# Banded attention: the query norm factors of groups 1 to 3 by a power on GpSimd and a Newton step on VectorE

## Chip, cores and metric

The kernel runs on one core of one Trainium2 chip. The metric is the device time of one execution in microseconds; the time before is the median of 3 runs. Engines are named as the profile names them: PE (TensorE matmul), PEld (its weight loads), DVE (VectorE), ACT (ScalarE), POOL (GpSimd), SP (SyncE).

## What is computed

The reference is two transformer blocks over 512 tokens of 1024 features: eight stages, four of them gated feed-forward layers. The change lies in the seventh stage, a sliding-window attention. It has 16 query heads and 2 key heads of 64 features, and blocks of 128 queries that read their own and the previous key block. Cut to what matters:

```python
def rms_norm_2(x, g):
    xf = x.astype(jnp.float32)
    y = xf * lax.rsqrt(jnp.mean(xf * xf, axis=-1, keepdims=True) + EPS)
    return (y * g.astype(jnp.float32)).astype(x.dtype)

def swa_layer(x, norm_g, w_in, q_g, k_g, sinks, w_out):
    proj = rms_norm_2(x, norm_g) @ w_in
    q, k, v = jnp.split(proj, ...)
    q = rms_norm_2(q.reshape(B, S, C_KV_HEADS, C_GROUP, C_HEAD_DIM), q_g)
    k = rms_norm_2(k.reshape(B, S, C_KV_HEADS, C_HEAD_DIM), k_g)
    o = sliding_window_attention(q, k, v, sinks).astype(x.dtype)
    return x + o @ w_out
```

`sliding_window_attention` is scores, plus a bias by distance, softmax with a learned sink in the denominator, times values. The norm factor of a query and head, one over the root of its mean square, enters as a factor on its scores.

## The kernel before

All engines run hand-written, fixed instruction streams that are tied by semaphores. Nothing is reordered: the order in which each engine's function issues its work is the order in which it runs. Every large product is computed in three passes (high by high, low by high, high by low parts), one "unit" of weights of 128x1024 being eight tiles, 24 matmuls, some 5.5 us of PE. A unit's weights are loaded by SP, rounded to the high part by ACT (line 176) and the rest is formed on POOL (line 187), three units ahead of use.

The class `WindowAttention` (from line 2070 on) holds the stage. Its units are k, q0, q1, v, q2 to q7 and then eight units of the output projection. The attention itself runs in 16 steps (`STEPS`): step n is query block n % 4 of group n // 4, and a group is 4 heads, that is, two q tiles. A step's work goes around the engines:

- PE `scores(n)` (line 2182), two steps ahead of the rest;
- DVE `maxima(n)`: a copy of the sinks in the first two blocks of a group (line 2363), scores times norm factor plus bias, 4 instructions (line 2367), the negated maximum (line 2372);
- ACT `exps(n)`: 4 exponentials with their sums (line 2279);
- DVE `share(n)`: reciprocals of the sums (line 2380);
- POOL `divide(n)`: 4 products with these (line 2434);
- PE `turn_p(n)`: transposes into banks 6 and 7 (line 2196), ACT `copy_turned(n)` (line 2289), PE `values(n)` (line 2209);
- ACT `upper(n)` and DVE `lower(n)`: high and low part of the result (lines 2296 and 2386).

`maxima(13)`, to take one, waits for nothing but the scores, `exps(11)` and what stands ahead of it on DVE: in step 12 of the loop DVE issues `maxima(13)`, behind `share(11)` and `lower(7)` of step 11. Between these steps PE runs the projections q4 to q7 in steps 1, 3, 5 and 7 (`PROJECTED`); from step 8 on there is no projection, and PE gets the first tiles of the output projection only at step 14.

The norm factors of a group's queries take these steps. ACT squares the two q tiles (line 2263). In step 1, 5 and 9 (`STATS`) PE sums the squares by `query_stats(g)` for group g = 1, 2, 3 (line 2166), in a bank of PSUM of its own for g = 1 and in the free half of the bank of `values(n - 3)` for g = 2 and 3. One step later ACT takes the root (`query_roots`, line 2270) between `copy_turned` and `upper`, and DVE the reciprocal (`query_rstd`, line 2350), the last thing ahead of `maxima(4g)` in the next step. Square root and exponential are in different tables of ACT, so each of the three roots has a table load ahead of it and another ahead of the exponentials that follow. Group 0 has the same steps ahead of the loop, behind a root that the keys need anyway.

Four stages have constants of their own (masks, biases), which ACT's DMA queue loads at the stage's start, with one semaphore for each stage.

## Time and profile before

| | |
|---|---|
| median of 3 runs | 2199.66 us (2197.24 to 2201.47) |
| the profiled execution | 2197.87 us |
| its span, first to last instruction | 2196.1 us |
| PE busy | 2172.5 us, 99% of the span |
| DVE, ACT, POOL busy | 903.8, 839.2, 943.4 us |
| chain that ended last | PE 97%, DVE 1%, ACT 1% |
| granted clock of PE, mean | 0.997 |
| 16 steps of the attention | about 1703 to 1803 us of the span |

The profile is one execution. The median of the runs lies 1.8 us above the profiled execution's time, and that 1.8 us above its span. A busy share is an average over stages with different limits: what one stage is bound by is read in the timelines of that stage. "Idle before" in a timeline is the idle time of that engine ahead of the instruction, with the instruction that ended it.

### The profile page before, as it was taken

What the parts mean: (1) busy time and instruction counts of PE and PEld (TensorE: products, weight loads), DVE (VectorE), ACT (ScalarE), POOL (GpSimd) and SP (SyncE); (2) the same over time, 40 slices, a digit from 0 to 9 for tenths busy, and PEclk for the clock granted to TensorE, in tenths of its full rate; (3) what the DMA queues carried; (4) which work ended last, traced back from release to release, by engine and by line L of the source; (5) the groups of instructions that cost most, each with busy time, mean ns of one, the idle gap of its engine ahead of it and who ended that gap; (6) DMA issues with size and microseconds to landing.
All of it is one profiled execution on the core that took longest, in us unless ns stands there. A gap on an engine that the chain in (4) does not pass through costs nothing.

```text
span 2196.1 us, 28893 instructions
## 1 busy us (share of the span) xinstructions
PE 2172.5 (99%) x10346; PEld 1787.0 (81%) x10346; DVE 903.8 (41%) x1275; ACT 839.2 (38%) x1236; POOL 943.4 (43%) x457
## 2 busy tenths in 40 slices
PE   8999999999999999999999999999999999999999
PEld 7888887788887888888887788888888778888887
DVE  5222222554625522222226855555322655555400
ACT  5222223423433422223334634444323655444421
POOL 3444444423472444444442334444544435444443
PEclk9999999999999999999999999999999999999999
DMA  5333333222352233333332123333333103333332
GB/s 187 98 96 96 96 106 113 79 75 68 106 165 66 77 106 96 96 96 103 108 128 65 34 86 96 96 96 96 106 107 132 53 18 105 97 100 98 96 115 77
DMA packets 58973, 210.25 MB, mean 96 GB/s; under 512 B 6800, under 2 KB 7568, under 8 KB 58512
## 3 DMA queue, kind: packets, MB, share of 16 engines
q1 hardware_dynamic: 57024, 202.33, 30.4%
q10 hardware_dynamic: 1872, 6.83, 0.8%
q8 instruction: 55, 0.90, 0.2%
q14 instruction: 22, 0.18, 0.0%
HBM read 207.05 MB, written 2.10 MB: 95 GB/s over the span
## 4 chain that ended last, share of the span: by engine, by line
PE 97%; DVE 1%; ACT 1%; issue 0%; DMA 0%; POOL 0%; SPq 0%; DVEq 0%; ACTq 0%
PE psum L234 29%; PE psum L236 29%; PE psum L235 29%; PE psum L258 1%; PE psum L260 1%; PE psum L259 1%; PE psum L1286 1%; PE psum L1311 1%; PE psum L2196 1%; PE psum L2182 1%; PE psum L2209 1%; PE psum L1674 0%; PE psum L2166 0%; PE psum L841 0%; PE psum L1694 0%
## 5 line engine op out<-in xcount | busy, mean ns | idle before, releaser
L187 POOL TENSOR_TENSOR w_lo<-w_raw,w_hi 128x1024 fp32r<-128x1024 f32 x375 | 903.5, 2416 | 1151.8 <-ACT w_hi L176 1151.6
L234 PE MATMUL psum<-x_hi,w_hi 128*128 128x512 f32 x1816 | 713.9, 393 | 7.7 <-DVE x_lo L295 6.7
L236 PE MATMUL psum<-x_hi,w_lo 128*128 128x512 f32 x1816 | 707.9, 390 | 0.0
L235 PE MATMUL psum<-x_lo,w_hi 128*128 128x512 f32 x1816 | 707.6, 390 | 0.0
L176 ACT ACTIVATE w_hi<-w_raw 128x1024 fp32r<-128x1024 f32 x378 | 393.3, 1054 | 529.9 <-PE psum L236 496.4
L234 PEld LDWEIGHTS psum<-x_hi,w_hi 128*128 128x128 f32 x1816 | 340.8, 188 | 85.2 <-issue 10.6
L236 PEld LDWEIGHTS psum<-x_hi,w_lo 128*128 128x128 f32 x1816 | 340.7, 188 | 72.7
L235 PEld LDWEIGHTS psum<-x_lo,w_hi 128*128 128x128 f32 x1816 | 341.0, 188 | 70.5 <-issue 0.5
L279 DVE SCALAR_TENSOR_TENSOR x<-psum,x 128x512 f32<-128x512 f32 x64 | 44.3, 692 | 366.8 <-PE psum L236 366.2
L234 PE MATMUL psum<-ffn_hidden_hi,w_hi 128*128 128x512 f32 x352 | 136.9, 389 | 0.0
L235 PE MATMUL psum<-ffn_hidden_lo,w_hi 128*128 128x512 f32 x352 | 136.9, 389 | 0.0
L234 PE MATMUL psum<-glu_hidden_hi,w_hi 128*128 128x512 f32 x352 | 136.9, 389 | 0.0
L235 PE MATMUL psum<-glu_hidden_lo,w_hi 128*128 128x512 f32 x352 | 136.9, 389 | 0.0
L236 PE MATMUL psum<-ffn_hidden_hi,w_lo 128*128 128x512 f32 x352 | 136.9, 389 | 0.0
L236 PE MATMUL psum<-glu_hidden_hi,w_lo 128*128 128x512 f32 x352 | 136.9, 389 | 0.0
L564 ACT ACTIVATE ffn_hidden_hi<-row_d 128x512 f32 (+1 forms) x44 | 27.8, 632 | 222.3 <-DVE row_d L623 222.3
L612 DVE TENSOR_TENSOR row_d<-psum,rstd 128x512 f32<-128x512 f32 x44 | 30.4, 692 | 193.2 <-PE psum L236 193.1
L295 DVE SCALAR_TENSOR_TENSOR x_lo<-x,columns,x_hi 128x512 fp32r<-128x512 f32 x56 | 89.9, 1611 | 47.2 <-ACT x_hi L324 47.2
L558 ACT ACTIVATE row_d<-row_b,columns 128x512 f32<-128x512 f32 x44 | 36.0, 819 | 126.5 <-DVE row_b L612 126.5
L612 DVE TENSOR_TENSOR row_b<-psum,rstd 128x512 f32<-128x512 f32 x44 | 30.4, 692 | 130.0 <-PE psum L236 129.9
L235 PEld LDWEIGHTS psum<-ffn_hidden_lo,w_hi 128*128 128x128 f32 x352 | 66.1, 188 | 13.8
L236 PEld LDWEIGHTS psum<-glu_hidden_hi,w_lo 128*128 128x128 f32 x352 | 66.1, 188 | 13.8
(316 smaller groups left out, 2518.7 us busy)
## 6 DMA issues: line engine op xcount, KB each, us to landing
w_raw<-in_stream SPq DMA_DIRECT2D x378, 512.0 KB, 3.6
swa_bias<-in_swa_bias ACTq DMA_DIRECT2D x1, 2048.0 KB, 9.8
out<-x SPq DMA_DIRECT2D x8, 256.0 KB, 4.5
ab_bias<-in_ab_bias ACTq DMA_DIRECT2D x1, 1792.0 KB, 7.4
x<-in_x_in SPq DMA_DIRECT2D x5, 256.0 KB, 7.4
xattn_mem<-in_mem ACTq DMA_DIRECT2D x1, 1024.0 KB, 5.0
x<-in_x_in ACTq DMA_DIRECT2D x3, 256.0 KB, 4.8
w_raw<-in_stream SPq DMA_DIRECT2D x2, 256.0 KB, 3.9
```

What stands on the lines that cost most here:

```text
L176: act.activation(self.w_hi[:, place % SPLIT_SLOTS, :], self.w_raw[:, place % RAW_SLOTS, :], ACT.Copy).then_inc(self.w_hi_ready, 1)
L187: pool.tensor_tensor(self.w_lo[:, split, :], self.w_raw[:, raw, :], self.w_hi[:, split, :].bitcast(F32), ALU.subtract).then_inc(self.w_lo_ ...
L234: pe.matmul(out, w_hi, hi[:, k0 + j, :], start=first and j == order[0], stop=False)
L235: pe.matmul(out, w_hi, lo[:, k0 + j, :], start=False, stop=False)
L236: mm = pe.matmul(out, w_lo, hi[:, k0 + j, :], start=False, stop=last and j == order[-1])
L258: pe.matmul(out, hi[:, k, rows], w_hi, start=start, stop=False, skip_group_check=True)
L259: pe.matmul(out, hi[:, k, rows], w_lo, start=False, stop=False, skip_group_check=True)
L279: own(dve, dve.scalar_tensor_tensor(c.x[:, m, :], y, factor, c.x[:, m, :], ALU.mult, ALU.add), c.x_updated, self.done(m))
L295: dve.scalar_tensor_tensor(c.x_lo[:, m, :], c.x[:, m, :], self.gain_column(m), c.x_hi[:, m, :].bitcast(F32), ALU.mult, ALU.subtract).then_ ...
L558: act.activation(out[:], row[:, PAD:PAD + T], ACT.Identity, bias=self.table(f"f_conv_b{self.conv}", f, part * FT), scale=self.table(f"f_co ...
L564: act.activation(self.tile(self.h_hi, f), self.row3(c.row_d), ACT.Copy).then_inc(self.hidden_hi_ready, 1)
L612: own(dve, dve.tensor_tensor(up_row, up_bank, c.rstd[:], ALU.mult), self.up_scaled, f + (self.done + 1))
```

## The change

Group 0 keeps its root. For groups 1 to 3, at the place where DVE took the reciprocal, DVE now copies the sums plus epsilon from PSUM to a tile (`sums`), ahead of `lower`. POOL raises that tile to the power of -1/2 (`query_powers`) behind `divide` of the same step. At the start of the next step DVE makes one Newton step of it in three instructions, each waiting for the one before (`query_rstd`), ahead of `maxima(4g)`. ACT's `query_roots` for these groups goes. `upper` of the bank that holds the sums now waits for PE's sums to be done, which `query_roots` did before, and PE's `query_stats` of groups 2 and 3 waits for the previous factors. A tile of 128x16 is filled with -0.5 once. The four stages' constants count on one semaphore (32, 48, 112 and 128 are the running totals at 16 for each DMA); the loads themselves stay where they are.

```diff
+STAGE_LANDED = {"mix": 32, "xattn": 48, "ab": 112, "swa": 128}
...
-        self.consts = sem("consts_landed")
+        self.consts = c.stage_landed
...
+            self.q_power = sb("q_power", [P, 2, 2 * TB])
+            self.q_sums = sb("q_sums", [P, 2, 2 * TB])
...
             if g < 2:
                 turns.take(pe, f"qstat{g}")
+            else:
+                pe.wait_ge(self.q_rstd_ready, g)
...
-        def query_roots(g):
-            act.wait_ge(self.stat_done, 2 * g + 3)
-            if g >= 1:
-                act.wait_ge(self.q_rstd_ready, g)
-
-            act.activation(self.q_root[:], self.stat_columns(g)[:, 0:4 * TB].rearrange("p (t c) -> p t c", t=2),
-                           ACT.Sqrt, bias=self.eps64[:]).then_inc(self.root_ready, 1)
+        def first_roots():
+            act.wait_ge(self.stat_done, 3)
+            act.activation(self.q_root[:], self.query_sums(0), ACT.Sqrt, bias=self.eps64[:]).then_inc(self.root_ready, 1)
...
             act.wait_ge(self.values_done, n + 1)
+            if n > 0 and n + 3 in self.STATS:
+                act.wait_ge(self.stat_done, 2 * self.STATS[n + 3] + 3)
...
-            if n - 1 in self.STATS:
-                query_roots(self.STATS[n - 1])
...
+        def sums(g, bank_of):
+            dve.wait_ge(self.stat_done, 2 * g + 3)
+            if bank_of >= 0:
+                dve.wait_ge(self.mixed_hi_ready, bank_of + 1)
+            own(dve, dve.tensor_scalar(self.q_sums[:], self.query_sums(g), HALF * EPS, None, ALU.add),
+                self.q_sums_ready, g)
...
+            else:
+                dve.wait_ge(self.root_ready, g + 2)
+                chain.own(dve, dve.tensor_tensor(rstd, self.q_sums[:], self.q_root[:], ALU.mult))
+                chain.own(dve, dve.scalar_tensor_tensor(rstd, rstd, -0.5, self.q_root[:], ALU.mult, ALU.mult))
+                own(dve, dve.scalar_tensor_tensor(rstd, rstd, 1.5, self.q_root[:], ALU.add, ALU.mult),
+                    self.q_rstd_ready, g + 1)
...
+        chain.own(dve, dve.memset(self.q_power[:], -0.5))
...
         for n in range(self.STEPS):
+            if n - 2 in self.STATS:
+                query_rstd(self.STATS[n - 2])
             if n + 1 < self.STEPS:
                 maxima(n + 1)
             if n == 0:
                 take("q3", self.q[:, 3, :])
             share(n)
+            if n - 1 in self.STATS:
+                sums(self.STATS[n - 1], n - 4)
             if n >= 4:
                 lower(n - 4)
-            if n - 1 in self.STATS:
-                query_rstd(self.STATS[n - 1])
...
+        def query_powers(g):
+            pool.wait_ge(self.q_sums_ready, g)
+            if g >= 2:
+                pool.wait_ge(self.q_rstd_ready, g)
+            pool.tensor_tensor(self.q_root[:], self.q_sums[:], self.q_power[:], ALU.pow).then_inc(self.root_ready, 1)
...
             divide(n)
+            if n - 1 in self.STATS:
+                query_powers(self.STATS[n - 1])
```

## Rows read from the trace of the kernel before

**Rows 1.** Busy time by engine and share of the span, of the page.

```profile
PE 2172.5 (99%) x10346; PEld 1787.0 (81%) x10346; DVE 903.8 (41%) x1275; ACT 839.2 (38%) x1236; POOL 943.4 (43%) x457
```

**Rows 2.** Window view: length, busy PE, PEld, DVE, ACT, POOL, PEclk, DMA share, GB/s.

```profile
1755.00:1770.00 15.00, 13.72 (x112) 11.57 (x112) 12.65 (x28) 13.10 (x39) 5.67 (x14) 0.77 0.13 36
...
1770.00:1785.00 15.00, 12.70 (x116) 9.71 (x114) 11.23 (x24) 13.30 (x46) 6.63 (x16) 1.00 0.01 2
```

**Rows 3.** Waits, 1680 to 1810 us: who waited for whom, total, times, longest.

```profile
PE psum L2196 <- ACT swa_p_turned L2289: 3.4, 3, 1.3
```

**Rows 4.** Window view, PE alone: length, busy (count), PEclk, DMA share, GB/s.

```profile
1763.00:1764.00 1.00, 1.00 (x6) 0.50 0.06 16
...
1770.00:1771.00 1.00, 1.00 (x13) 1.00 0.00 0
```

**Rows 5.** Timeline of ACT, third group's root: start, length, what, idle before.

```profile
1763.81 1.28 ACT L2270 ACT_TABLE_LOAD   x1
...
1765.11 0.27 ACT L2270 ACTIVATE swa_q_root<-psum,swa_eps 128x16 f32<-128x16 f32 x1
...
1765.67 1.28 ACT L2279 ACT_TABLE_LOAD   x1
...
1769.40 1.09 ACT L2289 ACTIVATE swa_p_turned<-psum 128x512 f32<-128x512 f32 x2 [0.35 <-PE psum L2196]
...
1770.63 0.41 ACT L2279 ACTIVATE swa_p<-swa_s,swa_negated 128x129 f32<-128x129 f32 x1
```

**Rows 6.** Timeline of DVE, same stretch, same columns.

```profile
1764.80 0.18 DVE L2380 RECIPROCAL swa_shares<-swa_sums 128x4 f32<-128x4 f32 x1
...
1766.22 0.25 DVE L2350 RECIPROCAL swa_q_rstd<-swa_q_root 128x16 f32<-128x16 f32 x1
...
1766.97 1.12 DVE L2367 SCALAR_TENSOR_TENSOR swa_s<-psum,swa_q_rstd,swa_bias 128x128 f32<-128x128 f32 x4
...
1768.13 0.69 DVE L2372 TENSOR_REDUCE swa_negated<-swa_s 128x4 f32<-128x516 f32 x1
...
1769.13 0.18 DVE L2380 RECIPROCAL swa_shares<-swa_sums 128x4 f32<-128x4 f32 x1 [0.31 <-ACT swa_p L2279]
...
1770.86 0.42 DVE L2386 TENSOR_TENSOR swa_mixed_lo<-psum,swa_mixed_hi 128x256 fp32r<-128x256 f32 x1 [1.55 <-ACT swa_mixed_hi L2296]
...
1771.32 0.17 DVE L2363 COPY swa_s<-columns 128x4 f32<-128x4 f32 x1
```

**Rows 7.** Timeline of POOL: the divisions behind the three groups' statistics.

```profile
1722.13 1.84 POOL L2434 TENSOR_SCALAR swa_p<-swa_p,swa_shares 128x256 f32<-128x256 f32 x4 [2.12 <-DVE swa_shares L2380]
...
1744.19 1.84 POOL L2434 TENSOR_SCALAR swa_p<-swa_p,swa_shares 128x256 f32<-128x256 f32 x4 [1.36 <-DVE swa_shares L2380]
...
1765.08 1.83 POOL L2434 TENSOR_SCALAR swa_p<-swa_p,swa_shares 128x256 f32<-128x256 f32 x4 [1.88 <-DVE swa_shares L2380]
```

**Rows 8.** Groups by line and form: busy us, mean ns of one, idle before.

```profile
L187 POOL TENSOR_TENSOR w_lo<-w_raw,w_hi 128x1024 fp32r<-128x1024 f32 x375 | 903.5, 2416 | 1151.8 <-ACT w_hi L176 1151.6
...
L2042 POOL TENSOR_TENSOR row_b<-row_a 128x512 f32<-128x512 f32 x4 | 4.2, 1038 | 48.7 <-DVE row_a L1864 48.7
...
L2045 POOL TENSOR_TENSOR row_b<-row_b,ab_counts 128x16 f32<-128x16 f32 x2 | 0.8, 384 | 0.2
...
L435 DVE COPY stat_mix<-psum 128x16 f32<-128x16 f32 x1 | 0.2, 177 | 3.5 <-PE psum L420 3.5
...
L436 DVE SCALAR_TENSOR_TENSOR stat_mix<-stat_mix 128x8 f32<-128x8 f32 x1 | 0.2, 166 | 0.0
```

**Rows 9.** Timelines of PE and DVE, what follows groups one and two.

```profile
1732.30 1.09 PE L2196 MATMUL psum<-ident,swa_p 128*128 128x128 f32 x8
...
1728.72 0.69 DVE L2346 TENSOR_TENSOR swa_q<-psum,rstd 128x512 f32<-128x512 f32 x1 [3.98 <-PE psum L236]
...
1729.45 1.18 DVE L2363 COPY swa_s<-columns 128x4 f32<-128x4 f32 x1
...
1753.07 0.69 DVE L2346 TENSOR_TENSOR swa_q<-psum,rstd 128x512 f32<-128x512 f32 x1 [3.05 <-PE psum L236]
```

More of the change, by code:

```diff
@@ L117, in __init__ @@
         self.spare = self.sb("spare", [P, STAGE_GAP])
-        self.consts_landed = self.sem("consts_landed")
+        self.consts_landed, self.stage_landed = self.sem("consts_landed"), self.sem("stage_landed")
         self.out_landed, self.columns_landed = self.sem("out_landed"), self.sem("columns_landed")
@@ L876, in tensor @@
         pe.wait_ge(self.turn_read.sem, 1)
-        pe.wait_ge(self.consts, 32)
+        pe.wait_ge(self.consts, STAGE_LANDED["mix"])
         pe.wait_ge(c.rstd_ready, norm.n + 1)
@@ L1133, in vector @@
                 self.v_ready, b + 1)
-        dve.wait_ge(self.consts, 32)
+        dve.wait_ge(self.consts, STAGE_LANDED["mix"])
         for s in range(4):
@@ L1243, in __init__ @@
         sem = lambda n: c.sem(f"xattn_{n}")
-        self.mem_landed, self.mem_hi_ready, self.mem_lo_ready = sem("mem_landed"), sem("mem_hi_ready"), sem("mem_lo_ready")
+        self.mem_landed, self.mem_hi_ready, self.mem_lo_ready = c.stage_landed, sem("mem_hi_ready"), sem("mem_lo_ready")
         self.mem_squared, self.mem_summed, self.mem_stat = sem("mem_squared"), sem("mem_summed"), sem("mem_stat")
@@ L1389, in scalar @@
         norm.scalar_root()
-        act.wait_ge(self.mem_landed, 16)
+        act.wait_ge(self.mem_landed, STAGE_LANDED["xattn"])
         act.activation(self.mem_squares[:], self.mem[:], ACT.Square).then_inc(self.mem_squared, 1)
@@ L1573, in __init__ @@
         sem = lambda n: c.sem(f"ab_{n}")
-        self.consts = sem("consts_landed")
+        self.consts = c.stage_landed
         self.v_by_vector, self.v_by_scalar = sem("v_by_vector"), sem("v_by_scalar")
@@ L1710, in tensor @@
                 knorm(0)
-        pe.wait_ge(self.consts, 64)
+        pe.wait_ge(self.consts, STAGE_LANDED["ab"])
         pe.wait_ge(c.final_rstd_ready, 1)
@@ L1963, in vector @@
         chain.own(dve, dve.memset(self.eps64[:], HALF * EPS))
-        dve.wait_ge(self.consts, 64)
+        dve.wait_ge(self.consts, STAGE_LANDED["ab"])
         pairs = self.lam_in[:].rearrange("p (a b) f -> p a b f", b=2)
@@ L2035, in windows @@
             turns.wait_read(pool, f"u{g}")
-            pool.wait_ge(self.consts, 64)
+            pool.wait_ge(self.consts, STAGE_LANDED["ab"])
             if g >= 1:
@@ L2102, in __init__ @@
         sem = lambda n: c.sem(f"swa_{n}")
-        self.consts = sem("consts_landed")
+        self.consts = c.stage_landed
         self.v_turned, self.v_ready = sem("v_turned"), sem("v_ready")
@@ L2106, in __init__ @@
         self.k_ready, self.q_rstd_ready = sem("k_ready"), sem("q_rstd_ready")
+        self.q_sums_ready = sem("q_sums_ready")
         self.scores_done, self.scores_read, self.max_ready = sem("scores_done"), sem("scores_read"), sem("max_ready")
@@ L2130, in stat_columns, with query_sums @@
         return self.turns.bank(f"values{n - 3}")[:, 2 * P:4 * P]
+    def query_sums(self, g):
+        return self.stat_columns(g)[:, 0:4 * TB].rearrange("p (t c) -> p t c", t=2)
     @staticmethod
@@ L2309, in scalar @@
         ahead("v")
-        query_roots(0)
+        first_roots()
         act.wait_ge(self.v_turned, 1)
@@ L2346, in take @@
             turns.read.own(dve, dve.tensor_tensor(out, turns.bank(name), c.rstd[:], ALU.mult))
-        def query_rstd(g):
-            dve.wait_ge(self.root_ready, g + 2)
-            own(dve, dve.reciprocal(self.q_rstd[:, 2 * g:2 * g + 2, :], self.q_root[:]), self.q_rstd_ready, g + 1)
-            if g < 2:
+        def sums(g, bank_of):
[4 more added lines that the diff above has]
+                self.q_sums_ready, g)
+            if g < 2:
+                turns.read.value += 1
+                dve.nop().then_inc(turns.read.sem, 1)
+        def query_rstd(g):
+            rstd = self.q_rstd[:, 2 * g:2 * g + 2, :]
+            if g == 0:
+                dve.wait_ge(self.root_ready, 2)
+                own(dve, dve.reciprocal(rstd, self.q_root[:]), self.q_rstd_ready, 1)
+            else:
[4 more added lines that the diff above has]
+                    self.q_rstd_ready, g + 1)
+            if g == 0:
                 turns.read.value += 1
@@ L2402, in vector @@
         query_rstd(0)
-        dve.wait_ge(self.consts, 16)
+        dve.wait_ge(self.consts, STAGE_LANDED["swa"])
         take("q2", self.q[:, 2, :])
```

## The prediction

> **What bounds the kernel now.** I read the busy shares of the page first: PE is busy for 99% of the span [rows 1], so over the kernel nothing is to be had off PE, and the most that a change elsewhere can return is the 23.6 us in which PE stood idle. Next come the windows of the attention stage, 1700 to 1800 us. PE is busy without a break to 1755; then it has 13.72 of 15 us and 12.70 of 15 us, while DVE is busy for 12.65 and 11.23 and ACT for 13.10 and 13.30 [rows 2]. So steps 8 to 15, which have no projection between them, run at the pace of the loop DVE, ACT, POOL, and the earlier steps at PE's. PE's idle time in these two windows is 1.28 + 2.30 = 3.58 us, of which the waits show 3.4 us behind ACT's copies of the turned probabilities [rows 3]. The granted clock falls there too: 0.50 in the microsecond from 1763, at the lower level (1.2 GHz), back at 1.00 by 1770 (2.4 GHz) [rows 4]; ahead of the fall PE had stood idle for 1.3 us [rows 3]. Last I read the timelines of ACT, DVE and POOL around the third group's root, line by line [rows 5 to 7], and only from these can the change be costed.
>
> **What goes.** Three times ACT loses a table load of 1.28 us, the root, and the load that brings the exponentials back. For the third group that is 1763.81 to 1766.95 less what `upper` takes in it, so 1.30 + 0.18 + 1.30 = 2.8 us [rows 5]; three groups give 8.3 us of ACT. The pairs of groups 1 and 2 lie beside the projections q5 and q7, where PE is at its full rate, and their going is worth nothing at the end. In the third group ACT can start `exps(11)` at 1764.8 instead of 1766.97 and ends it some 2.1 us earlier. That only pays if what needs it is held by it; the next paragraphs show what is late next. DVE loses a reciprocal of 0.25 us [rows 6].
>
> Ahead of the root's table load stands an instruction that ends at 1763.79, and the root follows 1.30 us after the load began [rows 5]: no drain is to be seen beside the 1.28 us. The Trainium skill, "ScalarE: Activation LUTs", section "What ACT_TABLE_LOAD costs", counts a drain of about 1380 ns beside the load; by it a pair would return 5.3 us and not 2.6. Neither sum reaches the end of the stage, for the reason given below, so the forecast is the same by both.
>
> **What comes.** On DVE one addition from PSUM of 128x16 and three products of 128x16, each waiting for the one before. Near rows are a copy of 128x16 from PSUM at 177 ns and a product of 128x8 at 166 ns [rows 8]; with 0.03 to 0.04 us between dependent instructions, as between 1766.22 + 0.25 and the next, I take 0.21 us each: 0.21 us ahead of `lower`, and 0.63 us ahead of `maxima(4g)`.
>
> On POOL the power, 128x16. The trace has no power. From below it is bounded by POOL's product of the same shape, 0.384 us. Its columns cost (2416 - 1038) / 512 = 2.7 ns each in a product, so 0.34 us of the 0.384 are fixed. From above I bound it by the longest instruction that POOL has, 2.42 us for 1024 columns [rows 8], which would be 130 ns for a column of the power, 48 times a product's. A power is a series of steps and not one, and not a product of 1024 columns either; I take X = 1.0 us (some 40 ns a column, 15 times a product's), nearer to the row of its own shape, and keep 0.38 and 2.42. It could be below or above both; above is the first rival. The power is queued behind `divide` of its step and ahead of nothing but the weight halves and the next `divide`. DVE waits for it at the start of the next step, and behind that wait stand `maxima(4g)`, `share`, `lower` and the take of the next projection: this is the new wait, and it takes the place of the wait for ACT's root.
>
> **Group 3, which counts.** `divide(10)` runs from 1765.08 to 1766.92 [rows 7]; the sum it needs is ready long before (PE's sums end at 1764.4, `upper(6)` at 1764.8, the addition at 1765.1). So the power ends at 1766.92 + X, the Newton step at 1766.92 + X + 0.06 + 0.63 = 1767.6 + X. Then `maxima(12)`: sinks 0.2, scores 1.16, maximum 0.72 [rows 6] = 2.08 us, to 1769.7 + X. In the trace the maximum was done at 1768.8, but it wasn't what `exps(12)` waited for: ACT stood behind `copy_turned(9)` at 1769.40, which waited for PE, and began `exps(12)` at 1770.63 [rows 5]. DVE goes on with `share(11)` 0.25 and `lower(7)` 0.46 and reaches `maxima(13)` at 1770.4 + X, against 1771.32 now [rows 6]. Both ways out have the same slack: the loop slips by X - 0.9. For X = 1.0 that is 0.1 us, for 0.38 it is nothing, since then `upper(7)` holds `lower(7)` as before, and for 2.42 it is 1.5 us. `divide(11)` moves from 1769.41 to 1771.0, and PE's `turn_p(11)` at 1774.1 has that in hand. So the 2.1 us that ACT gains in `exps(11)` is not lost to ACT but stands unused: `share(11)`, which waits for it now (0.31 us of idle time [rows 6]), is behind `maxima(12)` on DVE, and that waits for POOL.
>
> **Groups 1 and 2.** `divide(2)` ends at 1723.97, `divide(6)` at 1746.03 [rows 7]. With 0.06 + 0.63 + 2.08 + 0.21 = 2.98 us behind the power, DVE is through with `share` at 1726.95 + X and at 1749.0 + X. Its next work is the take of a projection, at 1728.72 and 1753.07, set by PE [rows 9]. That leaves 1.8 and 4.1 us for X. On ACT the exponentials of step 4 and a weight half (1.57 + 0.97) follow the maximum and stand ahead of `copy_turned(2)`: to 1729.3 + X, and 0.96 more to 1730.3 + X for PE's `turn_p(3)` at 1732.30 [rows 9], slack 2.0. For group 2 the same chain ends at 1751.3 + X against a copy at 1754.6, slack 3.3. So for X = 1.0 both are hidden by the projections; at 2.42 group 1 costs 0.6 us. Without that cover each would slip by its 2.8 us or so.
>
> POOL and DVE also get in each other's way: the sink copy of 128x4 at 1729.45 took 1.18 us [rows 9], and it ended when POOL's weight half (1728.24 + 2.36) did, where others took 0.17 [rows 6]. The three products read two tiles of SBUF. At their time POOL has ended the power and waits for `share`, so nothing is added; the fill of -0.5 stands where DVE waits for a projection.
>
> **Edits at nothing.** PE's new wait in `query_stats` is for a factor that is ready at 1725.7 and 1747.7, 14 us and more ahead. `upper` waits for PE's sums as the root did. The shared semaphore changes no load: the totals are those of stages in order on one queue, and DVE comes to its wait for the bias only behind the take of v, long after the load's issue at the stage's start; the page gives that load 9.8 us.
>
> **The sum.** Group 3 +0.1, groups 1 and 2 nothing, the rest nothing: 2197.9 + 0.1 = 2198.0 us for an execution like the profiled one, and the median 1.8 us above that: 2199.8 us. By the bounds of X the sum is 0.0 to +2.1 us. The clock's fall belongs to it too. Today it costs little, as ACT and DVE set the pace then; if it doesn't come, the changed loop is no faster, since DVE's part above has no PE in it.
>
> **Rivals.**
> - Slower, by the power's length. From X = 0.9 group 3 slips one for one, from 1.8 group 1, from 3.3 group 2: the place is always DVE at its wait, with `maxima(4g)` behind. It is over 0.2% (4.4 us) from X = 3.3 us: 2.4 + 1.5 + 0 = 3.9 for groups 3, 1 and 2, and what their slips push on makes up the rest. For X = 5: 4.1 + 3.2 + 1.7 = 9.0 us, 2209 us; from there 3 us for each us. For it speaks that nothing in the trace is a power, and that POOL needs 2.7 ns even for a column of a product; against it that a column would need 180 ns, 70 products. 0.19.
> - The first power alone is dear, as code that is used for the first time. From 1.8 us on group 1 pays; 6 us would be 4.2 us, 2204 us with group 3's 0.1, just within 0.2%. In the trace the first of the `divide` products, also a new kind for POOL, began 0.37 us after POOL was free: that speaks against. 0.06. The Trainium skill, "GPSIMD Engine Reference", section "Instruction dispatch", has a rule of this kind for freshly loaded code, with about 6 us.
> - The clock falls elsewhere. Today's low stretch of 7 us lies where PE isn't the bound. If the idle time at the end of the loop (2.3 us from 1777 on) is what brings it down, 7 us at half rate fall on the output projection, which is all PE: +3.5 us, 2203.4 us. For it: the steps shift by a fraction of a microsecond. Against: in the trace idle times of the same length at 1777 to 1781 brought no fall. 0.08, within 0.2%.
> - Faster by over 4.4 us: it would have to win back all 3.58 us of PE's idle time and more, so the loop's bound would have to be ACT's tables throughout, and DVE's chain above speaks against that. Less than that, 1 to 3 us (2197 to 2199), comes if DVE and ACT shift against each other better than I think. 0.05 for the first, 0.10 for the second.
> - The change doesn't do what it says: a table load is left, since squares and copies need another table. In the trace squares and copies stand between exponentials without a load. 0.01, same time.
>
> **How the numbers follow.** The forecast, 2199.8 us with 2198 to 2202 as its own range, has 0.51. A measurement of this kernel tells a change of about 0.2%, 4.4 us, from none. Within that: 0.51 + 0.10 + 0.08 + 0.01 + 0.05 of the first power's 0.06 = 0.75. Slower: 0.19 + 0.01 = 0.20. Faster: 0.05. The range is to hold 8 in 10: down to 2196, which takes in most of the smaller gains, and up to 2207, X = 4.2, which leaves out the longer powers.
>
> **What would show it.** In the changed profile: six table loads less on the lines of the exponentials and roots, and `exps(3)`, `exps(7)` and `exps(11)` right behind `upper`. The power's own row gives X, which everything hangs on: near 1 us if I am right. DVE's three products at some 0.2 us, the first with some 1.5 + X us of idle time before it in group 3, ended by POOL's power. `maxima(13)` within 0.3 us of where it is now, counted from `divide(10)`. PE's idle time in the stage near 3.6 us, and its first output tile at the same distance from the loop's step 8. Wrong would be: X above 3 us; an idle PE at steps 3 to 6; a stage shorter by more than 1 us.

## The result, and the profile after

The changed kernel takes 2205.42 us (median of 13 runs, 2201.73 to 2208.08); the kernel before, beside it on the same chips, takes 2199.29 us (13 runs, 2197.24 to 2202.12). The ratio is 1.0025, 95% interval 1.0019 to 1.0032: slower by 4.2 to 7.0 us, where I had forecast 2199.8 us and no change that can be told. The time lies in the stated range, 2196 to 2207, near its upper end, and outside 2198 to 2202, the range of the forecast itself. In the further experiments the changed kernel came out at 1.0019 (1.0010 to 1.0028) and 1.0022 (1.0011 to 1.0033). The sizes of DVE's and ACT's steps were right, that of POOL's wasn't.

The page of the changed kernel, first the span and then the busy times; the execution took 2203.59 us:

```profile
span 2201.4 us, 28903 instructions
...
PE 2174.7 (99%) x10346; PEld 1787.9 (81%) x10346; DVE 902.3 (41%) x1285; ACT 830.1 (38%) x1227; POOL 952.5 (43%) x460
```

ACT's busy time is 9.1 us less than in [rows 1], most of it the six table loads (7.7 us) and three roots (0.8 us); POOL's is 9.1 us more. The same windows of the attention stage as [rows 2] (length, busy PE, PEld, DVE, ACT, POOL, PEclk, DMA share, GB/s), with the stage starting 2.4 us later here:

```profile
1755.00:1770.00 15.00, 14.22 (x127) 11.53 (x126) 12.26 (x27) 12.65 (x43) 9.48 (x18) 0.89 0.13 36
...
1770.00:1785.00 15.00, 10.32 (x97) 7.69 (x97) 11.05 (x28) 9.86 (x32) 7.72 (x13) 0.96 0.00 1
```

PE stands idle for 0.78 + 4.68 = 5.46 us, against 3.58 before. The timeline of POOL says why (start, length, what, idle before), the three powers, and ahead of the third the division of its step:

```profile
1726.37 2.93 POOL L2470 TENSOR_TENSOR swa_q_root<-swa_q_sums,swa_q_power 128x16 f32<-128x16 f32 x1
...
1749.44 2.92 POOL L2470 TENSOR_TENSOR swa_q_root<-swa_q_sums,swa_q_power 128x16 f32<-128x16 f32 x1
...
1768.01 1.85 POOL L2463 TENSOR_SCALAR swa_p<-swa_p,swa_shares 128x256 f32<-128x256 f32 x4 [1.87 <-DVE swa_shares L2406]
...
1769.82 2.91 POOL L2470 TENSOR_TENSOR swa_q_root<-swa_q_sums,swa_q_power 128x16 f32<-128x16 f32 x1
```

A power of 128x16 takes 2.92 us. In the kernel before POOL had no longer instruction on the average [rows 8]. The answer to [rows 6] and [rows 9] is in DVE's timeline: the first product of the Newton step in each group, and the sink copy that begins `maxima(13)`:

```profile
1729.33 0.18 DVE L2373 TENSOR_TENSOR swa_q_rstd<-swa_q_sums,swa_q_root 128x16 f32<-128x16 f32 x1 [4.67 <-POOL swa_q_root L2470]
...
1752.46 0.18 DVE L2373 TENSOR_TENSOR swa_q_rstd<-swa_q_sums,swa_q_root 128x16 f32<-128x16 f32 x1 [3.95 <-POOL swa_q_root L2470]
...
1772.83 0.18 DVE L2373 TENSOR_TENSOR swa_q_rstd<-swa_q_sums,swa_q_root 128x16 f32<-128x16 f32 x1 [4.26 <-POOL swa_q_root L2470]
...
1776.23 0.17 DVE L2389 COPY swa_s<-columns 128x4 f32<-128x4 f32 x1
```

DVE stands for 4.67, 3.95 and 4.26 us with POOL's power as what ends it. In the kernel before the wait of group 3 for ACT was nothing: the reciprocal followed `lower(6)` at once [rows 6]. What PE had of it, in its timeline:

```profile
1735.76 1.06 PE L2206 MATMUL psum<-ident,swa_p 128*128 128x128 f32 x8 [0.97 <-ACT swa_p_turned L2295]
...
1774.85 1.14 PE L2192 MATMUL psum<-swa_k,swa_q 64*128 64x256 f32 x8 [1.48 <-DVE swa_s L2393]
...
1783.52 0.83 PE L2206 MATMUL psum<-ident,swa_p 128*128 128x128 f32 x4 [1.99 <-ACT swa_p_turned L2295]
```

and in the waits of the stage, where [rows 3] had 3.4 us and no row for the scores:

```profile
PE psum L2206 <- ACT swa_p_turned L2295: 4.6, 4, 2.0
...
PE psum L2192 <- DVE swa_s L2393: 1.5, 1, 1.5
```

PE waits at 1735.76 for the copy of step 2, which ACT now makes behind `exps(4)`; at 1774.85 for DVE's reading of the scores of step 12; and at 1783.52 it waits longer than before.

To measure the stage by itself I take the copy of the norm factor on DVE, which stands once ahead of the stage and once behind it. In the changed kernel:

```profile
1682.74 0.69 DVE L368 COPY rstd<-psum 128x512 f32<-128x512 f32 x1 [2.14 <-PE psum L360]
...
1850.08 0.69 DVE L368 COPY rstd<-psum 128x512 f32<-128x512 f32 x1 [5.54 <-PE psum L360]
```

In the kernel before the first was at 1680.31 us and the second here:

```profile
1844.73 0.69 DVE L367 COPY rstd<-psum 128x512 f32<-128x512 f32 x1 [5.54 <-PE psum L359]
```

So the stage is 167.34 us long against 164.42, and 2.43 us of the later start lie ahead of it, where nothing differs but the semaphore of the constants. Behind the stage there are 351.3 to 351.4 us in both. This length is the yardstick of the experiments.

### The profile page after: what moved, and what is told of

Same layout as the page of the kernel before. It is cut to its first block, busy times and chain, and to the rows that moved or that the text cites. A ratio compares the mean times of both kernels' runs of the same rounds, so it can differ in the third digit from the quotient of the medians.

```text
span 2201.4 us, 28903 instructions
## 1 busy us (share of the span) xinstructions
PE 2174.7 (99%) x10346; PEld 1787.9 (81%) x10346; DVE 902.3 (41%) x1285; ACT 830.1 (38%) x1227; POOL 952.5 (43%) x460
## 4 chain that ended last, share of the span: by engine, by line
PE 96%; DVE 2%; POOL 1%; ACT 0%; issue 0%; DMA 0%; SPq 0%; DVEq 0%; ACTq 0%; POOLq 0%
PE psum L235 29%; PE psum L237 29%; PE psum L236 29%; PE psum L259 1%; PE psum L261 1%; PE psum L260 1%; PE psum L1287 1%; PE psum L1312 1%; PE psum L1675 0%; DVE swa_s L2393 0%; PE psum L2219 0%; PE psum L842 0%; PE psum L2206 0%; PE psum L1695 0%; PE psum L849 0%
## 5 line engine op out<-in xcount | busy, mean ns | idle before, releaser
L235 PEld LDWEIGHTS psum<-ffn_hidden_hi,w_hi 128*128 128x128 f32 x352 | 66.1, 188 | 13.8
```

Source lines behind the costliest of these rows:

```text
L235: pe.matmul(out, w_hi, hi[:, k0 + j, :], start=first and j == order[0], stop=False)
```

## Experiments

Theory A: the loss is the power's length, at DVE's wait, with the slacks of the prediction (0.9, 1.8 and 3.3 us for groups 3, 1 and 2). Theory B: it is in the other edits. Theory C: longer idle times of PE bring more falls of its clock into the stage. All kernels, with their stage and the start of it:

| kernel | median us | ratio to before (95%) | stage us | starts at us |
|---|---|---|---|---|
| before, its two profiles | 2199.3; 2199.42 | | 164.42; 164.26 | 1680.3; 1684.3 |
| changed, its three profiles | 2205.42; 2204.68; 2204.26 | 1.0025; 1.0019; 1.0022 | 167.34; 166.94; 169.73 | 1682.7; 1684.2; 1680.5 |
| product for the power | 2198.97 | 1.0001 (0.9992 to 1.0010) | 163.90 | 1680.7 |
| two powers | 2210.55 | 1.0051 (1.0036 to 1.0066) | 175.42 | 1684.0 |
| semaphore alone | 2199.60 | 1.0005 (0.9996 to 1.0014) | 164.32 | 1682.2 |
| power ahead of the division | 2201.12 | 1.0009 (1.0000 to 1.0018) | 165.66 | 1682.7 |
| group 3 alone | 2201.67 | 1.0005 (0.9996 to 1.0014) | 166.40 | 1682.1 |
| group 1 alone | 2200.96 | 1.0003 (0.9994 to 1.0013) | 166.32 | 1684.2 |
| early group 3, wait at step 10 | 2201.44 | 1.0007 (0.9998 to 1.0016) | 166.27 | 1679.2 |
| early group 3, wait at step 11 | 2198.73 | 0.9997 (0.9988 to 1.0006) | 163.43 | 1682.1 |

The ratio and its interval are estimated from all executions beside each other and needn't be the quotient of two medians: for group 3 alone the medians are 2201.67 and 2199.58 us, a quotient of 1.0010.

### A product in the power's place

```diff
-            pool.tensor_tensor(self.q_root[:], self.q_sums[:], self.q_power[:], ALU.pow).then_inc(self.root_ready, 1)
+            pool.tensor_tensor(self.q_root[:], self.q_sums[:], self.q_power[:], ALU.mult).then_inc(self.root_ready, 1)
```

> The power on GpSimd is replaced by a product of the same two tiles, so the norm factors of groups 1 to 3 are wrong and nothing else is left out. The stage is taken from the copy of its own norm factor to the copy of the next stage's: 164.42 us before, 167.34 us in the changed kernel. If the length of the power is the cause (2.92 us in the changed profile, at DVE's wait), the product takes 0.4 us or less, DVE's Newton step starts 2.5 us earlier in each group, and the stage is back at 164.4 us give or take 0.7; the time is that of before, 2199 to 2200 us. If the loss comes from the other edits (four more instructions on DVE, the wait of the high parts, the shared semaphore), it stays: stage near 167, time near 2205 us. If the clock's falls are a thing of their own, the stage's length is back but the median stays 2 us or more above the kernel before.

This kernel leaves out the power, so its norm factors are not the reference's; it serves for the time alone. Ratio 1.0001, stage 163.90 us. The third product on POOL, and on DVE the first step that waits for it and the start of `maxima(13)`:

```profile
1766.93 0.22 POOL L2470 TENSOR_TENSOR swa_q_root<-swa_q_sums,swa_q_power 128x16 f32<-128x16 f32 x1
...
1767.26 0.18 DVE L2373 TENSOR_TENSOR swa_q_rstd<-swa_q_sums,swa_q_root 128x16 f32<-128x16 f32 x1 [1.56 <-POOL swa_q_root L2470]
...
1770.65 0.17 DVE L2389 COPY swa_s<-columns 128x4 f32<-128x4 f32 x1
```

All of the change is in this kernel but 2.7 us of each power, and all of the loss is gone. Theory B falls. The stage is 0.4 to 0.5 us shorter than before, with none of the six table loads on ACT and POOL's part short, but not all of that is the loads'. From the start of `divide(10)` to the sink copy of `maxima(13)` it is 5.53 us here and 6.24 and 6.03 us in the two profiles of the kernel before; it is 5.77 us in the kernel with group 1 alone below, which still has ACT's root and both its loads in group 3. That leaves at most 0.2 us for the loads, as the clock of that stretch differs too. Another 0.3 us come from a copy on DVE that isn't held up as long (0.36 for 0.68 us; see the third profile of the changed kernel), and 0.5 us are lost again in the output projection, where the clock is low from 1778.3 to 1781.8 us. Why the loads bring so little is in DVE's row: it waits for `divide(10)` and the product, 1.56 us, the 1.5 us + X of the prediction less some 0.2.

### Two powers instead of one

```diff
+            pool.tensor_tensor(self.q_extra[:, g - 1, :, :], self.q_sums[:], self.q_power[:], ALU.pow)
             pool.tensor_tensor(self.q_root[:], self.q_sums[:], self.q_power[:], ALU.pow).then_inc(self.root_ready, 1)
```

> A second power, into a tile that nobody reads, goes ahead of each of the three on GpSimd, so DVE waits for 5.8 us of powers. By the slacks read in the trace of the kernel before (0.9 us for group 3, 1.8 for group 1, 3.3 for group 2, each with slope one above it) the stage loses 4.9 + 4.0 + 2.5 = 11.4 us against before: stage near 176 us, time near 2211 to 2214 us. If the power's length were not what counts, doubling it would add little to 2205 us. If only group 3 counted, it would add 2.9 us, 2208 us.

Ratio 1.0051, 2210.55 us, stage 175.42 us: 11.0 us above before, where the slacks gave 11.4. The waits of PE in the stage have a new first row, for DVE's reading of the scores:

```profile
PE psum L2193 <- DVE swa_s L2394: 7.0, 2, 5.5
...
PE psum L2220 <- DVE swa_mixed_lo L2413: 2.6, 2, 2.4
```

Another 2.9 us of power cost 7.4 us more of stage (the mean of the changed kernel's three is 168.0), and 8.3 us more than the two of them whose clock stays up in the projection of q7 (167.1); the slacks give 11.4 - 3.1 = 8.3. So the loss isn't in proportion to the power but comes by group, as each slack is used up. This run could tell the three slacks from one group alone, which would have given 2208 us.

### The shared semaphore alone

```diff
+STAGE_LANDED = {"mix": 32, "xattn": 48, "ab": 112, "swa": 128}
...
-        self.consts = sem("consts_landed")
+        self.consts = c.stage_landed
...
-        dve.wait_ge(self.consts, 16)
+        dve.wait_ge(self.consts, STAGE_LANDED["swa"])
```

> The kernel before with the one shared semaphore for the four stages' constants and nothing else of the change. It moves no load and waits for nothing new: 2199.3 us, within 0.1% of before, stage 164.4 us. The rival, that part of the 6 us of the whole change comes from it (a different semaphore, waits on a running total), would give 2200.5 us or more, and a longer stretch ahead of the attention stage, where the changed profile was 1.9 us later than the one before.

Ratio 1.0005 with an interval that holds 1, stage 164.32 us. By itself its interval would allow up to 3 us; but the kernel with the product has the shared semaphore too, and that is at 1.0001 (0.9992 to 1.0010). The semaphore has no price that shows. For the later start in the first changed profile the expectation has 1.9 us; by the copy's rows it is 2.43, and what moves it is told below.

### The power ahead of the division

```diff
             divide(n)
-            if n - 1 in self.STATS:
-                query_powers(self.STATS[n - 1])
```

with the two removed lines ahead of `divide(n)`.

> On GpSimd the power goes ahead of the division of the same step instead of behind it. The sums are ready 0.1 us after the shares, so the factors come 1.8 us earlier in each group and the division 2.9 us later. If what costs is DVE's wait for the power, the stage gains most of 1.8 us in group 3 and 1.1 us in group 1, and the later division is hidden by PE's own order: stage near 165.0 us, time near 2201 us. If the division, with the transposes of PE behind it, is as late as the factors were, the stage stays at 167 us or goes above it, 2205 to 2206 us.

Ratio 1.0009, 2201.12 us, stage 165.66 us: between the two expectations, nearer the first; 0.4 us of it lie behind the loop, in the output projection, where the clock is low from 1782.0 to 1785.4 us. POOL's rows, the third power and the division behind it:

```profile
1767.19 2.91 POOL L2470 TENSOR_TENSOR swa_q_root<-swa_q_sums,swa_q_power 128x16 f32<-128x16 f32 x1 [2.07 <-DVE swa_q_sums L2358]
...
1770.09 1.85 POOL L2463 TENSOR_SCALAR swa_p<-swa_p,swa_shares 128x256 f32<-128x256 f32 x4
```

DVE's first two products, which begin at 1770.20:

```profile
1770.20 0.39 DVE L2373 TENSOR_TENSOR swa_q_rstd<-swa_q_sums,swa_q_root 128x16 f32<-128x16 f32 x1 [2.64 <-POOL swa_q_root L2470]
...
1770.62 0.42 DVE L2374 SCALAR_TENSOR_TENSOR swa_q_rstd<-swa_q_rstd,swa_q_root 128x16 f32<-128x16 f32 x1
```

They take 0.39 and 0.42 us where they took 0.18 with POOL at rest; POOL divides at this time. The third product and the sink copy take the same 0.42 and 0.43, so some 0.9 us of the 1.8 gained by the order is given back. The trace of the kernel before had such a row already: its sink copy at 1766.50 took 0.43 us while `divide(10)` ran. PE has no idle time at step 3 in this kernel: group 1 costs nothing with the power first.

### Group 3 alone, group 1 alone

```diff
+    POWERED = (3,)
...
-            if n - 1 in self.STATS:
-                sums(self.STATS[n - 1], n - 4)
+            if n - 1 in self.STATS and self.STATS[n - 1] in self.POWERED:
+                sums(self.STATS[n - 1], n - 4)
```

and so for the power and the Newton step; the other groups have ACT's root and the reciprocal. For the second kernel `POWERED = (1,)`.

> Only group 3 has the power and the Newton step, groups 1 and 2 have ACT's root and the reciprocal as before. The power of 2.92 us is 2.0 us longer than the slack of 0.9 us that I read for this group, so the stage is 166.4 us and the time about 2201 us. Should the loss of the whole change come from all groups alike, a third of it would show, stage 165.4. Should ACT's two table loads saved here be worth something, the stage would be below 166.

Stage 166.40 us, 2201.67 us, ratio 1.0005 (0.9996 to 1.0014). The stage is what X - 0.9 = 2.0 us gives, and the interval holds it; so small a loss can't be told from none by the times. In the rows it can: from `divide(10)` to the sink copy of `maxima(13)` it is 8.23 us here, 2.0 to 2.2 us more than before, with the clock low for as long in the loop (1764 to 1772 us) as in both profiles of the kernel before.

> Only group 1 has the power. The projection q5 covers 1.8 us of it by my reading (1.6 where ACT's copy stands behind its weight half), so 1.1 to 1.3 us are left: PE waits about 1.0 us ahead of the transposes of step 3, as in the changed profile, and what is lost there isn't made up by the steps behind it, since a projection follows: stage 165.5 us, time near 2200.3 us. If the loss at step 3 is made up later in the stage, the stage is 164.4 and the time that of before.

2200.96 us as expected, but the stage is 166.32 and not 165.5 us. PE waits for 0.97 us ahead of the transposes of step 3, as foreseen. What comes on top is in the windows of this kernel (columns as above), where the clock falls in the projection of q7 with PE busy throughout:

```profile
1740.00:1749.00 9.00, 9.00 (x68) 7.52 (x68) 5.63 (x11) 6.73 (x18) 4.22 (x5) 1.00 0.24 73
...
1749.00:1753.00 4.00, 4.00 (x30) 3.32 (x30) 2.85 (x9) 3.97 (x11) 1.89 (x5) 0.57 0.25 95
```

By the mean of 0.57 some 3.4 of these 4 us are at the lower level (1.2 GHz), 1.7 us of loss by that. The take of q7 begins 2.6 us later in the stage than before: 1.0 us of PE's wait and 1.5 us of the fall, which neither profile of the kernel before has at this place. Behind that take 0.6 us are won back, most of it in the copy on DVE that is shown below (0.17 us for 0.68), so the stage is 2.0 us longer and not 2.6. This made me form theory C anew: not longer idle time, but another place.

### The changed kernel again, and the kernel before again

> The changed kernel once more, for a second profile and the state of the clock in it. The first profile has the stage 2.92 us longer than before and 2.43 us more lie ahead of the stage, where no instruction differs and the clock fell at 391 us. If the stage's loss is the whole effect of the change, further runs lie 3 to 3.5 us above before, 2202 to 2203 us. If longer idle times bring more falls of the clock into the stage (in the first profile at 1767 and 1784 us), the stage is 1 to 3 us longer in this profile than in the first and the time stays near 2205 us.

> The kernel before under another label, for a second profile and as the yardstick of what a difference of nothing looks like: ratio 1.000 within 0.1%, stage 164.4 us if the clock falls in it as in the first profile, down to 163.9 us where it falls elsewhere. The stretch ahead of the stage was 1680.3 us in the first profile; 1679 to 1684 us in the others with the same instructions there. If it comes out between these, that stretch varies by itself and no change of it belongs to the changed kernel.

> The changed kernel a third time. The two profiles so far have its stage at 167.34 and 166.94 us, and the stretch ahead of it at 1682.7 and 1684.2 us. If that stretch is chance, this look can have it at 1679 to 1682 us, and the stage at 167 to 168 us. If the changed kernel is bound to have it late, it is again above 1682.5 us.

First the stretch ahead of the stage. PE's windows from 391 to 398 us (length, busy, PEclk, DMA share, GB/s), in the first profile of the changed kernel, in the first of the kernel before and in its second:

```profile
391.00:398.00 7.00, 7.00 (x16) 0.51 0.27 77
```

```profile
391.00:398.00 7.00, 7.00 (x31) 1.00 0.26 77
```

```profile
391.00:398.00 7.00, 7.00 (x16) 0.51 0.27 77
```

The clock falls there or not, in the same kernel: the kernel before starts its stage at 1680.3 or 1684.3 us, the changed one at 1682.7, 1684.2 or 1680.5. Such windows, 1 us each, over all that lies ahead of the stage account for the whole of it: PE is busy at the lower level for 3.4 us in the profile whose stage starts earliest, at 1679.2 us, and for 12.9 to 13.0 us in the three that start it at 1684.2 and 1684.3; the start less half of that time is 1677.4 to 1677.9 us in all thirteen profiles. Which of the places get a fall is not settled by the kernel, so the 2.43 us of the first comparison are none of the change's.

Then the stage. The second profile has 166.94 us, the third 169.73. The third, in windows with all engines' busy times as above:

```profile
1740.00:1745.00 5.00, 5.00 (x48) 4.34 (x48) 3.53 (x6) 1.70 (x4) 2.36 (x1) 1.00 0.18 25
...
1745.00:1749.00 4.00, 4.00 (x32) 3.26 (x28) 0.82 (x4) 2.68 (x10) 3.64 (x5) 0.57 0.28 107
...
1765.00:1773.00 8.00, 8.00 (x53) 7.13 (x53) 3.98 (x9) 4.82 (x20) 6.12 (x9) 0.57 0.01 2
```

PE is busy throughout the first two, and in the second it is at the lower level for 3.4 us: 1.7 us by that, and the take of q7 is 1.6 us later in the stage than in the other two profiles of the changed kernel, which have no fall there. Ahead of it PE has the idle time that is new with the change:

```profile
1733.50 1.06 PE L2206 MATMUL psum<-ident,swa_p 128*128 128x128 f32 x8 [0.95 <-ACT swa_p_turned L2295]
```

Eight profiles have the clock at full level all through 1735 to 1755 us: both of the kernel before, and those of the product, of the semaphore, of the power ahead of the division, of group 3 alone, and of both kernels with early statistics, none of which has that idle time. Of the five profiles that have it or a longer one (three of the changed kernel, group 1 alone, two powers) two show the fall. That is a hint and no proof, as the idle time ends over eleven microseconds ahead of the fall.

The third profile is longer by another 1.2 us, and this is not the clock of the loop but one copy on DVE, that of the sinks behind the take of q7. In the first profile of the kernel before, the first of the changed one and its third:

```profile
1753.80 0.68 DVE L2363 COPY swa_s<-columns 128x4 f32<-128x4 f32 x1
```

```profile
1757.23 0.17 DVE L2389 COPY swa_s<-columns 128x4 f32<-128x4 f32 x1
```

```profile
1756.56 1.41 DVE L2389 COPY swa_s<-columns 128x4 f32<-128x4 f32 x1
```

POOL's weight half ends at 1754.45 us in the first of these and at 1757.95 in the third, 0.03 and 0.02 us ahead of the copy's end; in the second it begins only at 1757.88, behind the copy. From the take of q7 to `divide(10)` it is 11.3 us and this copy in all three, 12.01, 11.51 and 12.74 us. From there to the sink copy of `maxima(13)` the third has 8.21 us and the other two of the changed kernel 8.22, so its 6.8 us at the lower level in the loop cost nothing. So 0.5 us of what the power costs are hidden in the first two profiles of the changed kernel, as the copy no longer meets the weight half, and 0.7 us are added to the third.

### Statistics of group 3 one step earlier

```diff
-    SQUARED = {0: [2, 3], 2: [4], 4: [5], 6: [6], 8: [7]}
-    STATS = {1: 1, 5: 2, 9: 3}
+    SQUARED = {0: [2, 3], 2: [4], 4: [5], 6: [6], 7: [7]}
+    STATS = {1: 1, 5: 2, 8: 3}
+    POWERED = (2, 3)
```

> A version meant to beat both: group 1 keeps ACT's root, groups 2 and 3 have the power, and the statistics of group 3 are taken one step earlier (q7 squared in step 7, summed in step 8), so that the power of 2.92 us runs behind the division of step 9 and is done at about 1767, 1.5 us ahead of where DVE wants the factors. ACT has no table load from step 3 on. If ACT's loads held the loop up in the last steps, this shows what they are worth: stage 162.5 to 164 us, time 2197 to 2199 us. If DVE's own work bounds the last steps, as the product in place of the power suggests (stage 163.9 us), nothing more is won: 164 us, within 0.1% of before.

2201.44 us, stage 166.27: a miss, by a fault of my own. With the statistics one step earlier the Newton step moved too, to the head of step 10, ahead of `maxima(11)`, which doesn't need it. DVE's row, and behind it PE's:

```profile
1764.60 0.18 DVE L2378 TENSOR_TENSOR swa_q_rstd<-swa_q_sums,swa_q_root 128x16 f32<-128x16 f32 x1 [4.26 <-POOL swa_q_root L2477]
...
1766.94 1.14 PE L2193 MATMUL psum<-swa_k,swa_q 64*128 64x256 f32 x8 [3.12 <-DVE swa_s L2398]
```

DVE stood for 4.26 us and PE for 3.12. The next kernel puts it right:

```diff
-            if n - 2 in self.STATS and self.STATS[n - 2] in self.POWERED:
-                query_rstd(self.STATS[n - 2])
+            if n in (7, 11):
+                query_rstd({7: 2, 11: 3}[n])
```

> The version with early statistics of group 3, with its one flaw taken out: there DVE waited for the power at the head of step 10, ahead of the maxima of block 11, which don't need it, and stood idle for 4.26 us. Here the wait and the Newton step stand at the head of step 11, right ahead of the maxima of block 12. The power ends at 1764.5 us of that profile, before DVE gets there, so no engine waits for it. If the loss is only where DVE stands before the power, the 4.3 us come back and part of them was loss against before: stage 163 to 164 us, time 2197.5 to 2199.5 us. If the tables' going from ACT is worth something once nobody waits for POOL, it is at the low end or below, stage 162.5. If DVE's own work sets the end of the loop, the stage is that of the product in place of the power, 163.9 us.

2198.73 us, ratio 0.9997 (0.9988 to 1.0006), stage 163.43 us, the shortest of all. Between these two kernels only the place of a wait on DVE differs, and the stage differs by 2.8 us. POOL's third power and the division that follows, DVE's first two products:

```profile
1764.76 2.92 POOL L2477 TENSOR_TENSOR swa_q_root<-swa_q_sums,swa_q_power 128x16 f32<-128x16 f32 x1
...
1767.66 1.84 POOL L2470 TENSOR_SCALAR swa_p<-swa_p,swa_shares 128x256 f32<-128x256 f32 x4
...
1767.77 0.39 DVE L2378 TENSOR_TENSOR swa_q_rstd<-swa_q_sums,swa_q_root 128x16 f32<-128x16 f32 x1 [0.62 <-POOL swa_q_root L2477]
...
1768.19 0.42 DVE L2379 SCALAR_TENSOR_TENSOR swa_q_rstd<-swa_q_rstd,swa_q_root 128x16 f32<-128x16 f32 x1
```

I had expected nobody to wait for POOL here. The power began at 1764.76, behind the division of step 9, and ended at 1767.68, and DVE stood for 0.62 us; then the division held it, again 0.39 and 0.42 us for a product of 0.18. Still, the stage is 0.9 us shorter than before, and that can't be told in the time. Most of it isn't the table loads' either: from the take of q7 to the last block's scores on DVE it is 25.20 us here and 25.19 us with the product, 26.24 and 26.03 us in the kernel before, but 25.52 us with group 1 alone, where group 3 has its root on ACT. And the clock, low for 6.8 us of the loop in both profiles of the kernel before, has no fall in this stage at all. It is no slower than the kernel before and not measurably faster: of the orders tried none wins anything that can be measured.

## Why the prediction was right, and where it was off

The measured time lies in the range, but not by the forecast's own working. That had no change, 2199.8 us with 2198 to 2202 about it, and each of the three comparisons has a loss clear of nothing (6.1, 5.1 and 4.6 us between the medians). The range held because it was drawn up to X = 4.2 us for the sake of the first rival; with X as it is, the same sum gives 2202.8 us, and the rest up to 2205.4 is in no term of it, so that the number fell inside is in part luck. Of the signs named, X is 2.92 us and not near 1, PE is idle at step 3, which was to be a sign of being wrong, and `maxima(13)` is 2.0 us later, counted from `divide(10)`, and not within 0.3. DVE's wait of 4.26 us is what 1.5 + X gives, 4.4, less some 0.2.

**That the tables' loads bring nothing.** Right. ACT's work fell by 9.1 us where 8.3 were counted, and with POOL's part short at most 0.2 us of the stage's gain can be put down to the loads. The step of the prediction, that DVE's `share(11)` stands behind `maxima(12)` and that behind POOL, is what DVE's row of 1.56 us in the kernel with the product shows.

**The power, X.** This is the term that was mis-sized: 1.0 us was taken, with 0.38 to 2.42 us as bounds from the nearest rows; 2.92 us it is, above both. The fault was to bound an unknown operation by the longest instruction of the trace, which has nothing to do with it. Per column it is (2.92 - 0.22) / 16 = 0.17 us, some 60 times the 2.7 ns of a product by the slope in [rows 8]. And the product of the same two tiles is 0.22 us, not 0.384. The rival "slower, by the power's length", with a chance of 0.19, named the mechanism, the place, and each group's slack; its point, 3.3 us for 4.4 us of loss, was put a little too high.

**Group 3: X - 0.9.** Right. From the start of `divide(10)` to the sink copy of `maxima(13)` it is 1771.32 - 1765.08 = 6.24 us in the kernel before [rows 6, 7] and 1776.23 - 1768.01 = 8.22 us in the changed one: 1.98 us more, for 2.92 - 0.9 = 2.0. The other two profiles of the changed kernel have 8.22 and 8.21 us, the second of the kernel before 6.03.

**Group 1: X - 1.8.** Right: PE's transposes of step 3 begin at 1735.76 instead of 1732.30 [rows 9], 3.46 us later, of which 2.43 are the later start of the stage: 1.0 us, for 1.1. The expectation for group 1 alone left open that it might be made up later; the take of q7 is still 1.0 us late.

**Group 2: nothing up to 3.3.** Right in the changed kernel: the loss at the take of q7 is still 1.0 us (1756.50 against 1753.07 [rows 9], less 2.43). Two powers, 5.8 us, went beyond it: there the take of q6 is 3.9 us later in the stage than before and that of q7 6.1 us, 2.2 us for the 2.5 that this slack gives.

**The sum.** With X as measured the formula gives 2.0 + 1.1 = 3.1 us. The stages of the profiles differ by 168.0 - 164.3 = 3.7 us on the mean (three and two profiles), and the rows account for each. Beside PE's 1.0 us and the 2.0 to 2.2 us behind `divide(10)` there is DVE's sink copy, 0.5 us shorter in two profiles of the changed kernel and 0.7 us longer in the third; the fall of the clock in the projection of q7, 1.6 us in the third; and a fall at the start of the output projection, 1783.8 to 1787.2 us, in the first, with 0.4 us more from the loop's end to the end of the stage. I had the falls as a rival of their own, with the output projection as their place, 3.5 us as their price and 0.08 as their chance; the one that came there cost a ninth of that, and the dear one lay elsewhere.

The times differ by more than the stages: the medians by 6.1, 5.1 and 4.6 us. Nearly every execution has its span and its mean granted clock on record. The 94 of the kernel before have a mean span of 2197.8 us, the 31 of the changed one 2202.5 us, 4.7 us more. Another 0.4 us lie outside the span: the time is 2.2 us above it in the changed kernel and 1.8 us in the one before. It is 2.2 us with the product too; what it is, no run shows. The mean clock is 0.9964 before and 0.9959 in the changed kernel. Among the executions of the kernel before the span is 2199.9 us at 0.995 and 2195.5 us at 0.998, which makes 0.8 us of that difference, an estimate. So 3.1 + 0.8 + 0.4 = 4.3 of 5.1 us are accounted for, and 0.8 us aren't. Why the changed kernel has more time at the lower level isn't shown. It isn't the semaphore or another edit, since the kernel with the product has them all.

**The first power is no dearer than the others**: 2.93 against 2.92 and 2.91 us. That rival is out. The Trainium skill, "GPSIMD Engine Reference", section "Instruction dispatch", has about 6 us more for the first call of freshly loaded code; the first power shows no such time, in its length or ahead of it, and whether it was such a call no run tells.

**DVE's new steps.** 0.17 to 0.18 us each and 0.21 from start to start, as taken. That nothing is added by POOL's being at work at the same time held for the three products in the changed kernel, and fell as soon as the order was changed (0.39 to 0.42 us).

## What to carry to other kernels

Work that leaves an engine for another one pays only if the other is not later with it: here ACT gained 9 us and the stage a few tenths of a microsecond at best, since DVE waits for the division on POOL anyhow. Read for each place the slack up to the next thing that waits; with three slacks the stage could be told to within half a microsecond for one power and for two, where the clock stayed up, and most of the error sat in the one length that no row showed. At half a microsecond a copy of 0.17 us on another engine counts too: before a difference of stages is put down to the change, it is split at instructions that both kernels have. An operation that the trace doesn't have is not bounded by the longest one that it has: give the range an upper end by asking from which length on the answer changes, and put a chance on that.

## What the runs showed of the hardware

- A power of two tiles of 128x16 on GpSimd takes 2.91 to 2.93 us, a product of the same tiles 0.22 us.
- A VectorE product of 128x16 with two inputs in SBUF, and a copy of 128x4, take 0.39 to 0.43 us instead of 0.17 to 0.18 while GpSimd runs its products of 0.48 us each. The copy takes up to 1.41 us when it begins under a GpSimd product of 128x1024, and ends 0.02 to 0.03 us behind it.
- The granted clock of TensorE falls to its lower level for 3.4 or 6.8 us at a few places that differ from execution to execution of one kernel. At 391 us it did so in 5 of 13 profiles, with TensorE busy all through the 5 us before. The start of the attention stage moved between 1679 and 1684 us with it, by half of the time that TensorE was busy at the lower level ahead.
- A fall at the start of the output projection cost 0.4 to 0.5 us in three profiles, one of the same 3.4 us in the projection of q7 1.5 to 1.6 us in two.
